# Gate pairs, the way back of xT, and the fox logits: three orders changed in a two-layer decoder kernel

## The reference

```
ada = c_act @ w_ada[layer] + b_ada[layer]          # c_act = silu(c); 6144 columns; kv_w_ada: 2048 more
h = rms_norm(x, gain) * (1 + scale) + shift
q, k, v, g = split(h @ ret_w_in)                    # g is the gate, 2048 columns
y = rms_norm(retention(rotary(q), rotary(k), v))
x = x + g1 * ((silu(g) * y) @ ret_w_out)
x = x + g2 * (square(relu(modulated(x) @ w_mlp_in)) @ w_mlp_out)
...
logits = q @ k.T * scale + f_cum[q] - f_cum[k]      # FoX, causal, per head
p = softmax(logits);  y = p @ v
x = x + g1 * ((sigmoid(og) * y) @ fox_w_out)
```

## Time and profile before

| | us |
|---|---|
| median of three runs | 3009.42 (3009.34 to 3011.91) |
| the profiled execution | 3017.87 |
| its span | 3016.3 |
| TensorE busy in it | 2926.3 |

### The profile page before, as it was taken

One profiled execution on the slowest core, in us unless ns is written; L12 is line 12 of the kernel. 1 busy time (PEld: TensorE's weight loads), 2 busy tenths in 40 slices (PEclk: granted clock), 3 DMA queues, 4 the chain that ended last, 5 costly groups with the idle time before them and its releaser, 6 DMA issues.

```text
span 3016.3 us, 33307 instructions
## 1 busy us (share of the span) xinstructions
PE 2926.3 (97%) x12924; PEld 2347.2 (78%) x12924; DVE 1796.1 (60%) x2200; ACT 1044.7 (35%) x1340; POOL 338.9 (11%) x486
## 2 busy tenths in 40 slices
PE   7999998789999999999999999999999999999999
PEld 5788876668777788888888787876766888888887
DVE  6665544445555977776766425335454787768673
ACT  5111132222223533343335424424344433333331
POOL 1000000000001100011102101112221200011110
PEclk8999999899999999999999999999999999999999
DMA  6566544473331354475431323445433244465431
GB/s 231 182 204 237 200 143 161 145 265 116 103 116 42 103 183 154 154 266 173 135 104 47 141 99 114 151 121 115 117 83 82 98 157 152 152 246 207 140 133 56
DMA packets 186862, 439.49 MB, mean 146 GB/s; under 512 B 12977, under 2 KB 74852, under 8 KB 186724
## 3 DMA queue, kind: packets, MB, share of 16 engines
q0 software_dynamic: 61616, 222.34, 22.2%
q1 hardware_dynamic: 125108, 215.26, 21.5%
HBM read 314.09 MB, written 123.34 MB: 145 GB/s over the span
## 4 chain that ended last, share of the span: by engine, by line
PE 85%; DVE 5%; DMA 5%; ACT 2%; issue 2%; SPq 0%; POOL 0%; DVEq 0%; ACTq 0%; POOLq 0%
PE ps L2514 6%; PE ps L2515 6%; PE ps L2516 6%; PE ps L2676 6%; PE ps L2678 6%; PE ps L2674 6%; PE ps L2352 4%; PE ps L2351 4%; PE ps L2348 4%; PE ps L2806 3%; PE ps L2308 3%; PE ps L2314 3%; PE ps L2311 3%; PE ps L2440 3%; PE ps L2443 3%; PE ps L2444 3%
## 5 line engine op out<-in xcount | busy, mean ns | idle before, releaser
L2674 PE MATMUL ps<-z_hi,w_hi 128*128 128x512 f32 x768 | 298.8, 389 | 0.0
L2676 PE MATMUL ps<-z_lo,w_hi 128*128 128x512 f32 x768 | 298.8, 389 | 0.0
L2678 PE MATMUL ps<-z_hi,w_lo 128*128 128x512 f32 x768 | 298.8, 389 | 0.0
L2514 PE MATMUL ps<-h_hi,w_hi 128*128 128x512 f32 x576 | 231.7, 402 | 44.6 <-DVE stage L1699 36.7
L2515 PE MATMUL ps<-h_lo,w_hi 128*128 128x512 f32 x576 | 229.8, 399 | 0.0
L2516 PE MATMUL ps<-h_hi,w_lo 128*128 128x512 f32 x576 | 229.6, 399 | 0.0
L2348 PE MATMUL ps<-z_hi,w_hi 128*128 128x512 f32 x512 | 203.4, 397 | 0.0
L2352 PE MATMUL ps<-z_hi,w_lo 128*128 128x512 f32 x512 | 199.5, 390 | 0.0
L2351 PE MATMUL ps<-z_lo,w_hi 128*128 128x512 f32 x512 | 199.3, 389 | 0.0
L1503 DVE TENSOR_TENSOR w_lo<-w_raw,w_hi 128x2048 fp32r<-128x2048 f32 x52 | 119.0, 2289 | 115.2 <-ACT w_hi L981 115.2
L1519 DVE SCALAR_TENSOR_TENSOR misc<-misc,c_act 128x1024 f32<-128x1024 f32 x84 | 107.8, 1284 | 132.9 <-DMA misc<-w_ada 101.6
(11 more groups left out here) (379 smaller groups left out, 6574.3 us busy)
## 6 DMA issues: line engine op xcount, KB each, us to landing
t_s<-misc POOLq DMA_DIRECT2D x28, 1792.0 KB, 6.9
misc<-t_s POOLq DMA_DIRECT2D x98, 512.0 KB, 4.2
misc<-w_ada SPq DMA_DIRECT2D x80, 512.0 KB, 5.1
w_raw<-w_mlp_in SPq DMA_DIRECT2D x32, 1024.0 KB, 5.5
w_raw<-ret_w_in SPq DMA_DIRECT2D x24, 1024.0 KB, 7.4
x_s<-xT SPq DMA_DIRECT2D x12, 1024.0 KB, 6.6
xT<-x_s SPq DMA_DIRECT2D x12, 1024.0 KB, 9.5
a_bufs<-w_mlp_out SPq DMA_DIRECT2D x12, 1024.0 KB, 22.6
```

The lines of the kernel that those rows point to most:

```text
L2514: MM(out, hi, b_hi[:, k, :], start=k == 0 and i in (0, 1, 3), stop=False, skip_group_check=True)
L2674: MM(bank[at + m], hi, ring_b(z_hi, slot)[:, cols], start=first and i not in (2, 4, 5), stop=False, skip_group_check=True)
L2676: MM(bank[at + m], hi, ring_b(z_lo, slot)[:, cols], start=False, stop=False, skip_group_check=True)
L2678: mm = MM(bank[at + m], lo, ring_b(z_hi, slot)[:, cols], start=False, stop=last, skip_group_check=True)
```

## The change

Three edits, none of which adds or removes a transfer or an arithmetic instruction.

1. In the gate stage, SyncE asks for the first two modulation tiles of a pair ahead of load_gate(q + 2), and for the other two behind it (chunk 9, before the stage, keeps its order). VectorE takes the second two tiles of a pair at the end of the pair's work, behind the block sums, the cuts and the three gate_add, instead of between the sums' first and second cut.
2. SyncE waits for ret_second_loaded before it issues the four transfers that bring xT back.
3. In the FoX heads the logits of block n + 2 are issued where those of n + 1 were, and a head begins with the logits of blocks 0 and 1.

```diff
@@ SyncE
-            for i, (w_a, col_a) in enumerate([(w_ada[1], 3072), (w_ada[1], 4096), (w_ada[1], 5120), (kv_w_ada, 0),
-                                              (kv_w_ada, 1024)]):
-                for j in range(2):
-                    if i < 4:
-                        load_gate(2 * i + j)
-                    else:
-                        sp.wait_ge(split_lo_done, in_split(0, NG - 2 + j, 3))
-                        load_pair(W_RET + j, j, out_pair(ret_w_out, 0, j), first=True)
-                    for k in range(4 * j, 4 * j + 4):
-                        ada_load(i + 9, k, w_a, col_a)
+            for j in range(2):
+                load_gate(j)
+                for k in range(4 * j, 4 * j + 4):
+                    ada_load(9, k, w_ada[1], 3072)
+            for q in range(NG):
+                w_a, col_a = ((w_ada[1], 4096), (w_ada[1], 5120), (kv_w_ada, 0), (kv_w_ada, 1024))[q // 2]
+                k0 = 4 * (q % 2)
+                for k in range(k0, k0 + 2):
+                    ada_load(10 + q // 2, k, w_a, col_a)
+                if q + 2 < NG:
+                    load_gate(q + 2)
+                else:
+                    j = q + 2 - NG
+                    sp.wait_ge(split_lo_done, in_split(0, q, 3))
+                    load_pair(W_RET + j, j, out_pair(ret_w_out, 0, j), first=True)
+                for k in range(k0 + 2, k0 + 4):
+                    ada_load(10 + q // 2, k, w_a, col_a)
             sp.wait_ge(c_added, added(0, NG - 1, 3))
+            sp.wait_ge(ret_second_loaded, 48)
@@ VectorE, loop over q
                     gate_low(q + 1, 0)
-                for k in range(4 * (q % 2) + 2, 4 * (q % 2) + 4):
-                    ada_tile(chunk, k)
                 if q + 1 < NG:
                     gate_low(q + 1, 1)
                 for n in range(3):
@@
                 else:
                     prep(W_RET, 0)
+                for k in range(4 * (q % 2) + 2, 4 * (q % 2) + 4):
+                    ada_tile(chunk, k)
@@ TensorE, loop over the FoX heads
                 logits(h, 0)
+                logits(h, 1)
                 for n in range(NF):
-                    if n + 1 < NF:
-                        logits(h, n + 1)
+                    if n + 2 < NF:
+                        logits(h, n + 2)
```

## The result

| | before | after |
|---|---|---|
| median of the runs, us | 3010.44 (3009.34 to 3011.91) | 2970.77 (2961.21 to 2972.29) |
| the profiled execution, us | 3017.87 | 2972.29 |
| its span, us | 3016.3 | 2970.7 |

The ratio is 0.9861 (95% interval 0.984 to 0.9883): faster, by 39.7 us of the medians and 45.6 us of the two profiled spans. I predicted 2967, with a range of 2949 to 2994.

What follows compares the result with a forecast made beforehand. TensorE, busy 97% of the span, was taken as the bound, so only its waits and lower clock counted. Gains of 44.4 (gate pairs) + 1.9 (xT) - 4 (FoX) = 42.3 us, carried over to the median, gave 2967 us, range 2949 to 2994.

Steps and rivals of the forecast that it cites:

- gate_add in time: Gate stage: with 5.5 us tile loads gate_add comes 2.7 us before it is needed, so TensorE's waits for it go.
- B: Rival: gate pairs become bound by the loop of tile loads; 29 us lost at 13 us loads, 2996 us; chance 0.15.
- D: Rival: gate waits only exchanged, gate_add waiting for late gate spills; within 6 us of before; chance 0.04.
- E: Rival: slower, tile loads past 16.3 us make gate pairs longer than today's 27.1 us; 3026 us; chance 0.04.
- The column sums: Gate stage: column sums after pairs 1, 3, 5 and 7 newly wait 2.2 us each for late tiles, 8.8 us.
- The clock behind them: Gate stage: the granted clock falls after the column sums' waits, three falls at 1.8 us, 5.4 us lost.
- The reserve: Gate stage and retention head 0: 3 us allowed for a late tile or spill and head 0's first operands.
- xT: Retention head 0: delaying xT's four 1 MB loads removes TensorE's wait for rv, 1.9 us gained.
- The FoX heads: FoX heads: logits issued two blocks ahead lose 4 us in all, between 6 gained and 12 lost.
- the new wait for the row transfers: FoX heads: each next head's first logits wait for the q<-low_tiles rows, 0.5 us 13 times, 6.5 us lost.
- Rival C: FoX row transfers held up in every head as after head 0, 15 us lost, 2982 us; chance 0.12.
- F: Rival: column sums wait half, clock holds, no reserve needed, FoX loses nothing; 59 us gained, 2950 us; chance 0.05.

Runs made afterwards that it cites:

- x11: Kernel after, with the third logits group behind the first score tile in FoX head 0 alone; 2966.1 us, ratio 0.9847.
- x2: Kernel before, with only the wait for ret_second_loaded ahead of xT's return added; 3007.6 us, ratio 0.9991.
- x1: Kernel before, with both gate edits (SyncE's and VectorE's order) and nothing else; 2966.5 us, ratio 0.9851.
- x3: Kernel before, with only the FoX logits issued two blocks ahead; 3006.9 us, ratio 0.9997.
- x6: Kernel after, with the last two modulation tiles of a pair ahead of the third cut; 2954.3 us, ratio 0.9803.
- x10: Kernel after, with the column sums of pairs 1, 3 and 5 behind the next pair's first product; 2956.9 us, ratio 0.9809.
- x4: Kernel before, with only SyncE's new queue order in the gate stage, VectorE's order old; 2954.1 us, ratio 0.981.
- x9: Kernel after, with each FoX head's third logits behind its first score tile and the last two tiles behind the pair's first gate_add; 2943.3 us, ratio 0.9769.
- x5: Kernel before, with only VectorE's new order in the gate stage, SyncE's queue old; 2990.6 us, ratio 0.9929.
- x8: Kernel before, with SyncE's new gate order, the xT edit and FoX logits two ahead, third group behind the score tile; 2948.7 us, ratio 0.9785.

## Why the prediction held, and where it did not

- **What could be had.** Forecast 61.6 us. The stage before was 222.0, and 159.5 is all work at the upper clock: 62.5.
- **gate_add in time.** Right. Its chain rested on tile loads of 5.5 us; in pair 1 the two loads were used 3.9 and 6.1 us after they were issued (448.2 to 452.09, 449.6 to 455.73). VectorE ends at T + 21.3, forecast T + 21.2. The spills had landed: VectorE has no wait for g_s in the stage. So B, D and E did not come about. In E one bound is miscounted: the loop of L + 11.6 passes the 27.1 us of a pair at L = 15.5, not at 16.3. Its price and its chance do not rest on that.
- **The column sums.** Forecast four waits of 2.2, 8.8 us; measured 2.27, 2.27, 1.97 and 2.85, together 9.4.
- **The clock behind them.** Forecast 5.4 us as three falls of four; in the 6 us behind each of the four sums it was 0.54, 0.70, 0.72 and 0.77, and the time at the lower clock in the stage, added up over 2 us windows, is worth 8.9 us. This term was too small by 3.5 in this trace. The same gate code in x11 loses 5.1 (mean clock 0.97 over its 175.9 us), so the size of this term differs from one trace to the next.
- **The reserve.** Forecast 3 us; head 0's first operands cost 0.4. The gate stage gained 42.6 for 44.4 forecast.
- **xT.** Forecast 1.9, and between the traces head 0 does get 1.9 us shorter (42.59 to 40.71), but that agreement is luck. The term took the wait for rv as one that only the xT edit removes. It removes it on the kernel before (2.1 us in x2); the gate edits remove it too (x1, 41.0 us, no wait for rv), since head 0's operands are then asked for earlier. Between before and after head 0 lost the wait for rv (1.9) and one of 0.9 us for ScalarE, and at a mean clock of 0.965 it gave 1.4 us back.
- **The FoX heads.** Forecast 4 us lost, measured nothing lost or gained. The step that failed is the new wait for the row transfers, 13 times 0.5, 6.5 us. I took the 3.80 us from transpose to logits for the time that the rows need and the order would only shorten what covers it; in fact the rows are there within 3.15 us, TensorE's idle time there is 0.26 us, and it was 0.24 before: 0.02 us a head in place of 0.5. The second step that failed hides it in the sum: in head 0 I put 0.6 us for the exp behind its table load, and it was 2.0 us of waiting and 3.4 us of low clock. What I gave to the transpose and the head's end, 8.2 us, fits as a remainder, and no run measured it by itself: the waits for exp (5.4) and head 0's clock (3.4) make 8.8, and the total moved by less than 0.1. Errors of 6.5 us one way and 4.8 the other cancelled in good part; that the term came within 4 us is luck. With the clock held up (x3) the same edit gained 3.3 us of trace.
- **Rival C** failed with that step. The Trainium skill, DMA: Bandwidth & Descriptors, section on queues, rings and completion order, has the increment wait for the engine's earlier writes. It speaks of writes ahead. The loads of head h + 3 are issued behind the rows, a step earlier than before, and the rows were still used 3.15 us after the transpose in 14 of 14 heads: they did not hold them up. Behind head 0 the loads are issued ahead of the rows (in the kernel before from 2009.33 on, the rows from 2019.40 on). In seven of the thirteen traces the rows came late there, with 0.57 to 1.43 us of idle time at the weight load, and in all seven the last of those loads landed 1.9 to 3.6 us after the first row was asked for. In the kernel after, x6 and x10 it had landed before that, in x2 and x3 1.7 and 1.8 us after it, and the rows were on time; x1 is the exception, with 2.9 us and rows on time. So the traces agree with the rule for loads ahead of the rows, and nothing in them speaks for loads behind.
- **What was not seen.** I priced the two gate edits as one. The idle 8.31 and 1.82 us of VectorE were those of the tile loads, and asking earlier was enough to take them out of gate_add's way; VectorE's new order then only bought the column sums' waits and the clock behind them. Taking it out (x4) is 13 us of the stage better. I had listed the column sums as what is late next and did not ask which of the two edits makes them late. F, with 57.2 of its 59 us in the stage, had 164.8 for it; x4 has 166.2 and x9 162.0, so F was not the end of what could be had.
- **Absolute time.** I carried 8.5 us from profiled execution to median; after, that difference was 1.5, the profiled run being the slowest of four. The stretch ahead of the gate stage, the same code everywhere, takes 421.2 to 428.9 us in the thirteen traces, and from head 0's output to FoX it is 1307.5 to 1310.6, with different falls of the clock in them. Spans differ by 45.6 us and medians by 39.7, and the sum of my terms, 42.3, lies between; such spreads are large enough for the gap of 5.9, but no run shows which of them made it. In the stretch ahead of the gate stage they go with the clock: its mean is 0.99 in x5 (421.2 us) and 0.96 in x8 (428.9).

What stays open: why the wait of 2.0 us in FoX head 0 brings the clock down in the kernel after, x6 and x10 and not in x3, and what makes the clock fall more or less often in the stretch ahead of the gate stage. No run here was made for either.

## What to carry to other kernels

When a change moves a load and the consumer's place together, price each alone: here the earlier load alone was worth 55.8 us of the stage (x4) and the moved consumer alone 20.4 (x5), while both together, at 42.6, made the next reader late. A piece of work moved out of one deadline's way has a deadline of its own; put it where its engine waits anyway (behind the first gate_add here) and not at the end. An instruction moved ahead by one step in a loop should be followed in the first pass too, where a table load can make its releaser later than in the pattern, 2.0 us of waiting here instead of 0.35.

## What the runs showed of the hardware

- A short wait with one-column matmuls at its side can cost clock on top of its length. Four column sums behind waits of 2.0 to 2.9 us lowered the granted clock to between 0.54 and 0.77 in the 6 us that followed: 9.4 us of waiting, and 8.9 us of clock in the stage. Three sums of x6 did so behind waits of 0.65 us or less.
- 16 matmuls of 128x1 alone do not do it: the first three sums of x9 and of x10, with no wait, left the clock at 1.00. A wait behind the sum seems to act like one ahead of it: the fourth sum of x9 did not wait, head 0's 1.54 us for rv_first followed it, and the clock was 0.72 in the next 6 us. Waits of that length without such matmuls, 1.87 us in head 0 before and 2.37 in x3, left it at 1.00.
- The same wait does not always act alike: 2.0 us in head 0 of FoX was followed by 7 us at 0.51 in the kernel after, at 0.53 in x6 and x10, and by 1.00 in x3.
- Two 512 KB loads issued one behind the other were used 3.9 and 6.1 us after their issue (pair 1, after). With 1 MB issued ahead of them VectorE stood idle for 8.31 us before it could use the first (pair 2, before). The order within one queue, alone, took 55.8 us from the eight pairs (x4), the clock that it gave back included.
